# Cache copies moved to a later phase, the last layer norm rewritten, and a projection split between the first attention units

## The chip, the cores and the metric

The kernel runs on one core of a Trainium2 chip. The metric is the device time of one execution in microseconds (us). TensorE (PE) does the matrix products, VectorE (DVE) and ScalarE (ACT) work on rows, GpSimd (POOL) does a little of both and issues DMAs, and SyncE (SP) only issues DMAs. Each engine has its own instruction stream, worked off in order. They meet at semaphores: `wait_ge` holds the stream of its engine until the count is reached.

## The reference

One inference step of a decoder layer, for 1024 prompt rows and 64 sample rows (8 sequences of 8) of width 1024. Cut to what matters here:

```
q, k, v, u, c_b, g_a, g_c = mixer_projections(x, pos, w_in)      # z = x W_in; rotary q, k
A   = dilated_band_attention per group (128,1), (512,4), (2048,16), groups weighted by their denominators
Cv  = c_b * conv3(u)
mix = (sigmoid(g_a) * (A W_pa) + sigmoid(g_c) * (Cv W_pc)) W_out
h   = layer_norm(alpha * x + mix);   y = layer_norm(alpha * h + peer_ffn(h))
new_kv_sample[g] = concat(cache_g, new k/v)[-n_prev:]            # the old rows are moved up by 8
```

The last line matters: of each sample cache (3 groups: 128, 512 and 1024 rows per sequence) all rows but the first 8 are copied unchanged, DRAM to DRAM. That is 52.5 MB.

## The kernel before

The program is a chain of phases, each closed by a barrier over all engines: `load_x`, `prompt_attn`, `sample_attn`, `conv_gates`, `branches`, `mix_ln1`, retrieval, `build_gates`, `experts`, `ln2_out`. Products of the projections are exact to fp32: each factor is split into a high and a low part (ACT writes the high part, DVE the low one), and `split3` (L59 to L61) issues three matmuls for one product.

`prompt_attn` runs over four slices `s` (two heads of each of three groups). In a slice PE first projects: ri = 0, 1, 2 are v, k and q, each for nine row tiles t = 0..8; tile 8 (`PT`) holds the 64 sample rows. A projection is 24 matmuls into one of three PSUM banks, and DVE rotates it (`rotate`: L374, L376, L380) or keeps it; PE turns the prompt tiles (L469). After all 27 projections come 32 units (N: group 0, R: groups 1 and 2). Unit u on PE is `scores` (L483), `turn_probs` (L493), `weigh_values` (L506), issued as scores(u+2), turn_probs(u), weigh_values(u-1). DVE masks the scores (L389) and keeps the outputs (L396), ACT does the exponentials (L308) and copies the turned probabilities (L316). After unit 8 ACT and DVE also split the weights of the next slice (`split_w(s + 1, 0)`: ACT L289 twice, DVE L359 twice); ACT waits there for the load `w_raw`, which SP issues (L223) once the k rows of this slice are stored. So a late `w_raw` holds ACT, and with it the exponentials that PE needs.

The cache copies are DMAs on POOL's queue (L277): two in slice 0, one in slice 1 and one in slice 2, each issued when the slice's last weights are split. Nothing waits for them but the end of the program. The profile calls POOL's DMA queue q0 (software_dynamic) and SP's q1 (hardware_dynamic).

`conv_gates` works through 40 units of weights, five kinds times eight. SP loads `c_raw` (L828, 512 KB for a unit, in pieces of 512 bytes, two buffers); ACT and DVE split it (L854, L884); PE multiplies, 72 matmuls a unit. Unit 0 can't start without the first load, and the next phases can't start before the last unit. POOL stores the finished gates (L840) and gives their buffers free.

`ln2_out` runs over nine row tiles. DVE adds and takes the statistics (L1123, L1127, L1129), ACT the root (L1133), DVE centres and scales (L1139), POOL multiplies by the gain and adds the bias (L1144, L1146) and issues the store (L2108); then POOL itself waits for the store to land before it takes the next tile. Tiles 4 to 8 are first copied to `f_stage` and transposed.

## Time and profile before

| what | value |
|---|---|
| median of 3 runs | 4798.47 us (4792.62 to 4831.89) |
| the profiled execution | 4800.55 us, span 4799.0 us |
| PE busy | 3962.5 us (83%) |
| DVE busy | 3043.2 us (63%) |
| ACT busy | 1179.5 us (25%) |
| POOL busy | 1759.1 us (37%) |
| mean granted TensorE clock | 0.889 of full speed |

The granted clock is 1.00 (2.4 GHz) or 0.50 (1.2 GHz) at any moment; a value between is a mean over a stretch. The busy shares are means over phases with different limits, so the stages that the change touches are read one by one. In the rows below, a timeline row has the start, the length, the engine and line, and in brackets the idle time before it with what ended it; x6 is a count; "PEld" is the loading of weights. A windows row has the stretch and its length, then busy time and count for PE, PEld, DVE, ACT and POOL, then PE's granted clock, the busy share of the 16 DMA engines, and GB/s.

The chain that ended last reaches back only through the last phase, since each phase is closed by a barrier.

### The profile page before, as it was taken

How to read it: one execution, taken by the hardware profiler on the slowest of the kernel's cores; microseconds unless marked ns; L12 is line 12 of the kernel's file. 1: busy time of each engine (PE TensorE's matmuls, PEld its weight loads, DVE VectorE, ACT ScalarE, POOL GpSimd, SP SyncE). 2: the span in 40 equal slices, each digit the busy share in tenths (PEclk: the TensorE clock that was granted, in tenths of full speed). 3: DMA queues.
4: the chain of work that ended last, by engine and by line, in shares of the span. 5: the costliest groups of instructions: out<-in, count | busy, mean ns of one | idle time of the engine just before them, and what ended most of it. 6: DMA issues, size and time to landing. Idle time of an engine off the chain costs nothing. (4 is left out here: it accounts for less than half of the span.)

```text
span 4799.0 us, 64513 instructions
## 1 busy us (share of the span) xinstructions
PE 3962.5 (83%) x24889; PEld 3686.0 (77%) x24889; DVE 3043.2 (63%) x5862; ACT 1179.5 (25%) x2121; POOL 1759.1 (37%) x1228
## 2 busy tenths in 40 slices
PE   7897979798999897798066489888888888888882
PEld 7796969657999896687055488888888888888882
DVE  3332323212222234399888699989998999999984
ACT  1212121311111101143289122222222222222221
POOL 0000000000000002377500566666766666666644
PEclk8787879899999999888589699999999999999996
DMA  5433332252111244110024899999999999999973
GB/s 154 152 99 122 108 113 65 78 218 73 59 60 60 85 130 141 56 31 10 0 124 193 333 359 357 355 350 362 360 355 358 348 359 359 356 356 354 358 271 112
DMA packets 470701, 982.63 MB, mean 205 GB/s; under 512 B 49022, under 2 KB 267518, under 8 KB 467427
## 3 DMA queue, kind: packets, MB, share of 16 engines
q0 software_dynamic: 156704, 619.52, 34.6%
q1 hardware_dynamic: 312578, 355.11, 21.8%
q8 instruction: 166, 2.72, 0.2%
q10 hardware_dynamic: 1152, 4.46, 0.2%
q14 instruction: 101, 0.82, 0.1%
HBM read 901.43 MB, written 131.28 MB: 215 GB/s over the span
## 5 line engine op out<-in xcount | busy, mean ns | idle before, releaser
L1879 POOL DMA_INDIRECT u_row<-in_peer_u_dram,eid x512 | 785.1, 1533 | 703.1 <-DVE dots L1938 417.7
L59 PE MATMUL e_ps<-coef_h,v_h 128*128 128x288 f32 x2048 | 661.3, 323 | 243.6 <-DVE v_l L1907 199.4
L59 PE MATMUL e_ps<-hBh,u_h 128*128 128x288 f32 x2048 | 607.4, 297 | 62.8 <-DVE u_l L1900 62.8
L1954 DVE SCALAR_TENSOR_TENSOR f_row<-v_row,g_coef,f_row 128x1024 f32<-128x1024 f32 x508 | 650.9, 1281 | 6.1 <-DMA v_row<-in_peer_v_dram,eid 5.6
L1885 POOL DMA_INDIRECT v_row<-in_peer_v_dram,eid x512 | 573.1, 1119 | 197.4 <-issue 154.2
L59 PEld LDWEIGHTS e_ps<-coef_h,v_h 128*128 128x128 f32 x2048 | 414.8, 203 | 298.1 <-DVE v_l L1907 244.9
L60 PE MATMUL e_ps<-coef_l,v_h 128*128 128x288 f32 x2048 | 634.4, 310 | 0.0
L61 PE MATMUL e_ps<-coef_h,v_l 128*128 128x288 f32 x2048 | 632.1, 309 | 0.0
L1938 DVE CUSTOM_DVE_ANT_0 u_row<-u_row,h_row 128x1024 f32<-128x1024 f32 x512 | 620.9, 1214 | 10.1 <-DMA u_row<-in_peer_u_dram,eid 10.0
L61 PE MATMUL e_ps<-hBh,u_l 128*128 128x288 f32 x2048 | 607.0, 296 | 0.0
L60 PE MATMUL e_ps<-hBl,u_h 128*128 128x288 f32 x2048 | 606.9, 296 | 0.0
L59 PEld LDWEIGHTS e_ps<-hBh,u_h 128*128 128x128 f32 x2048 | 388.0, 189 | 63.7 <-DVE u_l L1900 63.7
L60 PEld LDWEIGHTS e_ps<-coef_l,v_h 128*128 128x128 f32 x2048 | 415.6, 203 | 0.0
L61 PEld LDWEIGHTS e_ps<-coef_h,v_l 128*128 128x128 f32 x2048 | 414.0, 202 | 0.0
L60 PEld LDWEIGHTS e_ps<-hBl,u_h 128*128 128x128 f32 x2048 | 388.0, 189 | 0.0
L61 PEld LDWEIGHTS e_ps<-hBh,u_l 128*128 128x128 f32 x2048 | 387.8, 189 | 0.0
L59 PE MATMUL c_ps<-xTh,c_wh 128*128 128x384 f32 (+1 forms) x960 | 317.1, 330 | 18.1 <-DVE c_wl L884 18.1
L61 PE MATMUL c_ps<-xTh,c_wl 128*128 128x384 f32 (+1 forms) x960 | 316.3, 329 | 0.0
L60 PE MATMUL c_ps<-xTl,c_wh 128*128 128x384 f32 (+1 forms) x960 | 316.2, 329 | 0.0
L1839 ACT ACTIVATE v_h<-v_raw 128x512 fp32r<-128x512 f32 x256 | 160.3, 626 | 624.1 <-PE e_ps L61 624.1
L281 POOL DMA_DIRECT2D s_att<-attS x4 | 2.3, 571 | 763.3 <-ACT attS L327 763.3
L840 POOL DMA_DIRECT2D s_gate<-gate x16 | 8.5, 531 | 709.6 <-ACT gate L871 709.6
(282 smaller groups left out, 8469.9 us busy)
## 6 DMA issues: line engine op xcount, KB each, us to landing
u_raw<-in_peer_uT_dram SPq DMA_DIRECT2D x128, 512.0 KB, 9.0
v_raw<-in_peer_vQ_dram SPq DMA_DIRECT2D x256, 256.0 KB, 8.5
s_g<-gate_block SPq DMA_DIRECT2D x9, 4096.0 KB, 11.2
x_gate<-s_g SPq DMA_DIRECT2D x64, 576.0 KB
out_o_kv_sample_dram<-in_cache_kv_w_dram POOLq DMA_DIRECT2D x2, 16256.0 KB, 94.6
c_raw<-in_w_in_dram SPq DMA_DIRECT2D x40, 512.0 KB, 3.8
w_raw<-in_w_in_dram SPq DMA_DIRECT2D x96, 192.0 KB, 3.7
cache_v<-in_cache_vS_dram SPq DMA_DIRECT2D x8, 2304.0 KB
```

The source lines that it names most:

```text
L59: pe.matmul(out, lh, rh, start=first, stop=False)
L60: pe.matmul(out, lh, rl, start=False, stop=False)
L61: return pe.matmul(out, ll, rh, start=False, stop=last)
L281: pool.dma_start(io["s_att"][s][:, :SEQ], attS[:]).then_inc(att_out, 16)
L840: pool.dma_start(io["s_gate"][x][j], gate[:, x]).then_inc(gate_out[x], 16)
L1839: act.activation(vh[:, n % 2], vraw[:, n % VR], ACT.Copy).then_inc(v_hi, 1)
L1879: pool.indirect_dma_start(urow[:, r % RING], None, io["peer_u"][0], bass.IndirectOffsetOnAxis(ap=eid[:, r:r + 1], axis=0)).then_inc(urow_i ...
L1885: pool.indirect_dma_start(vrow[:, r % RING], None, io["peer_v"][0], bass.IndirectOffsetOnAxis(ap=eid[:, r:r + 1], axis=0)).then_inc(vrow_i ...
L1938: dve.tensor_tensor_reduce(urow[:, r % RING], urow[:, r % RING], hrow[:, t % 2], 1.0, 0.0, ALU.mult, ALU.add, dots[:, s % 2, x:x + 1]).the ...
L1954: dve.scalar_tensor_tensor(out=f, in0=vrow[:, r % RING], scalar=coef[:, s % 2, x:x + 1], in1=f, op0=ALU.mult, op1=ALU.add).then_inc(weighe ...
```

## The change

Three things.

The cache copies leave `prompt_attn`. All four are issued by POOL, one after the other, as its first act in `conv_gates`. The gate stores there are issued by ACT on its own DMA queue; POOL only waits for them and frees the buffers.

`ln2_out` is written anew. Tiles 4 to 8 come first. All 13 loads are issued ahead, into a buffer for every tile. PE forms alpha * h + f in PSUM, with a scaled identity and the identity (so the transposes of tiles 4 to 8 are part of the sum). DVE takes the statistics from PSUM and does the rest with two `scalar_tensor_tensor` (centre and gain; scale and bias). ACT takes the roots and issues the stores, and waits for them once, at the end. POOL has nothing to do.

In `prompt_attn` the q projection of the sample tile has PSUM bank 7 to itself, and comes in two halves of 12 matmuls: before the turn of q tile 7, and before weigh_values(0). The first scores come between the last prompt projections, and DVE rotates the sample tile after unit 3's step. The outputs of the units have two banks instead of three.

```diff
-    OBANK = (7, 3, 4)
+    OBANK = (3, 4)
+    RING = ZT - 1
...
+        def z_bank(s, ri, t):
+
+            return 7 if (ri, t) == (2, PT) else (s * RING + ri * NT + t) % 3
+
+        def s_bank(s, u):
+            return (s * RING + 2 * NT + PT - SR + u) % SR
...
         def _(pool):
             for s in range(SP):
-                pool.wait_ge(w_lo_done, s * 6 + 6)
-                for g, a, b in ((0, 0, 120), (1, 0, 504)) if s == 0 else ((2, (s - 1) * 508, s * 508),) if s < 3 else ():
-                    pool.dma_start(io[f"o_kv{g}_sample"][0, :, a:b].rearrange("b r w s2 e -> b (r w s2 e)"),
-                                   io[("cache_kv_w128", "cache_kv_w512", "cache_kv_w2048")[g]][0, :, DS + a:DS + b]
-                                   .rearrange("b r w s2 e -> b (r w s2 e)")).then_inc(k["cache_moved"], 16)
                 pool.wait_ge(at_done, 2 * (s + 1))
                 pool.dma_start(io["s_att"][s][:, :SEQ], attS[:]).then_inc(att_out, 16)
...
                     for t in range(PT):
+                        if ri == 2 and t >= PT - 2:
+                            exp(s, t - (PT - 2))
                         copy_turn(s, ri, t)
-                exp(s, 0)
                 for u in range(NU):
-                    if u + 1 < NU:
-                        exp(s, u + 1)
                     copy_probs(s, u)
+                    if u + 2 < NU:
+                        exp(s, u + 2)
...
-                    for t in range(NT):
+                    for t in range(NT if ri == 1 else PT):
                         if t < 2:
                             dve.drain()
+                        if ri == 2 and t == PT - 1:
+                            mask_scores(s, 0)
                         rotate(s, ri, t)
...
-                mask_scores(s, 0)
                 mask_scores(s, 1)
-                for u in range(NU):
+                mask_scores(s, 2)
+                for u in range(1, NU):
                     if u + 2 < NU:
                         mask_scores(s, u + 2)
-                    if u >= 1:
-                        keep_out(s, u - 1)
+                    keep_out(s, u - 1)
+                    if u == 3:
+                        rotate(s, 2, PT)
                     if u == 8 and s + 1 < SP:
                         split_w(s + 1, 0)
...
+            def project(s, ri, t, rows=range(KD)):
                 n, zi = rows_of(t), z_of(s, ri, t)
                 if zi >= 3:
-                    pe.wait_ge(z_free, zi - 2)
+                    pe.wait_ge(z_free, zi - (3 if ri == 0 and t < 3 else 2))
...
+                else:
+                    pe.wait_ge(z_free, z_of(s, 2, PT - SR + u) + 1)
...
-                if u >= 3:
-                    pe.wait_ge(o_kept, s * NU + u - 2)
-                if u == 1:
-                    pe.wait_ge(turn_free, (s + 1) * 2 * PT)
+                if u >= 2:
+                    pe.wait_ge(o_kept, s * NU + u - 1)
+                else:
+                    pe.wait_ge(turn_free, (s + 1) * 2 * PT - 1 + u)
...
+                    for t in range(NT if ri < 2 else PT):
                         project(s, ri, t)
                         if ri == 0 and t == 5 and s >= 1:
                             join(s - 1)
...
                             pe.wait_ge(at_done, 2 * s)
                         if ri >= 1 and t >= 1:
                             turn(s, ri, t - 1)
-                pe.wait_ge(z_free, z_of(s, 2, NT - 1) + 1)
-                scores(s, 0)
-                scores(s, 1)
-                for u in range(NU):
+                        if ri == 2 and t >= PT - 2:
+                            scores(s, t - (PT - 2))
+                project(s, 2, PT, range(KD // 2))
+                turn(s, 2, PT - 1)
+                turn_probs(s, 0)
+                scores(s, 2)
+                project(s, 2, PT, range(KD // 2, KD))
+                weigh_values(s, 0)
+                turn_probs(s, 1)
+                scores(s, 3)
+                for u in range(2, NU):
                     if u + 2 < NU:
                         scores(s, u + 2)
                     if units[u][0] == "R" and units[u - 1][0] == "N":
                         pe.wait_ge(vp_in, 16 * (s + 1))
                     turn_probs(s, u)
-                    if u >= 1:
-                        weigh_values(s, u - 1)
+                    weigh_values(s, u - 1)
                 weigh_values(s, NU - 1)
...
             pool.sem_inc(gate_free, 2)
+            for g, a, b in ((0, 0, 120), (1, 0, 504), (2, 0, 508), (2, 508, 1016)):
+                pool.dma_start(io[f"o_kv{g}_sample"][0, :, a:b].rearrange("b r w s2 e -> b (r w s2 e)"),
+                               io[("cache_kv_w128", "cache_kv_w512", "cache_kv_w2048")[g]][0, :, DS + a:DS + b]
+                               .rearrange("b r w s2 e -> b (r w s2 e)")).then_inc(k["cache_moved"], 16)
             with pool.Fori(0, KD) as j:
-                for x in range(2):
-                    pool.wait_ge(z_act, j * AJ + ((2 + x) * NC + AJ))
-                    pool.dma_start(io["s_gate"][x][j], gate[:, x]).then_inc(gate_out[x], 16)
                 for x in range(2):
                     pool.wait_ge(gate_out[x], (j + 1) * 16)
                     pool.sem_inc(gate_free, 1)
...
+                    if m >= 3:
+                        act.wait_ge(z_act, q * (2 * AJ) + (i // NU * AJ + (m - 1) * NC + AJ))
+                        act.dma_start(io["s_gate"][m - 3][bass.ds(q * 2 + i // NU, 1)].rearrange("o p n -> (o p) n"),
+                                      gate[:, m - 3]).then_inc(gate_out[m - 3], 16)
...
+    ORDER = tuple(range(GTILES, NT)) + tuple(range(GTILES))
+    NY = 4
...
+            for i, t in enumerate(ORDER):
+                n = rows_of(t)
+                sp.dma_start(H[:n, t], io["s_h"][t * P:t * P + n]).then_inc(h_in[t], 16)
                 if t < GTILES:
+                    sp.dma_start(F[:, t], io["s_f"][t * P:(t + 1) * P]).then_inc(h_in[t], 16)
...
+        @block.tensor
+        def _(pe):
+            pe.wait_ge(alpha_ready, 1)
+            for i, t in enumerate(ORDER):
+                n = rows_of(t)
+                if i >= NY:
+                    pe.wait_ge(centred, i - NY + 1)
+                pe.wait_ge(h_in[t], 32 if t < GTILES else 16)
+                for a in range(2):
+                    cols = slice(a * 512, (a + 1) * 512)
+                    pe.matmul(ps[:n, i % NY, cols], scaled_id[:n, :n], H[:n, t, cols], start=True, stop=False)
+                    if t < GTILES:
+                        m = pe.matmul(ps[:n, i % NY, cols], k["ident"][:], F[:, t, cols], start=False, stop=True)
+                    else:
+                        for j in range(4 * a, 4 * a + 4):
+                            m = pe.matmul(ps[:n, i % NY, j * P:(j + 1) * P], k["acc"][:, j, t * P - TA:t * P - TA + n],
+                                          k["ident"][:], start=False, stop=(j % 4 == 3))
+                m.then_inc(y_ready, 1)
...
+            def stats(i):
+                n, x = rows_of(ORDER[i]), i % 2
+                dve.wait_ge(y_ready, i + 1)
+                for a in range(2):
+                    dve.bn_stats(st[:n, x, 6 * a:6 * a + 6], ps[:n, i % NY, 512 * a:512 * (a + 1)])
+                dve.drain()
+                dve.bn_aggr(mv[:n, x], st[:n, x]).then_inc(var_ready, 1)
+
+            def finish(i):
+                t, x = ORDER[i], i % 2
+                n = rows_of(t)
+                dve.wait_ge(std_ready, i + 1)
+                dve.reciprocal(rstd[:n, x:x + 1], std[:n, x:x + 1])
+                dve.scalar_tensor_tensor(out=H[:n, t], in0=ps[:n, i % NY], scalar=mv[:n, x, 0:1], in1=gain[:n],
+                                         op0=ALU.subtract, op1=ALU.mult).then_inc(centred, 1)
+                dve.drain()
+                dve.scalar_tensor_tensor(out=H[:n, t], in0=H[:n, t], scalar=rstd[:n, x:x + 1], in1=bias[:n],
+                                         op0=ALU.mult, op1=ALU.add).then_inc(done, 1)
+
+            stats(0)
+            dve.wait_ge(consts, 32)
+            for i in range(NT):
+                if i + 1 < NT:
+                    stats(i + 1)
+                finish(i)
...
+            def root(i):
+                n, x = rows_of(ORDER[i]), i % 2
+                act.wait_ge(var_ready, i + 1)
+                act.activation(std[:n, x:x + 1], mv[:n, x, 1:2], ACT.Sqrt, bias=eps[:n]).then_inc(std_ready, 1)
+
+            def store(i):
+                t = ORDER[i]
+                dst = io["o_y_prompt"][0, t * P:(t + 1) * P] if t < PT else io["o_y_sample"].rearrange("b s d -> (b s) d")
+                act.wait_ge(done, i + 1)
+                act.dma_start(dst, H[:rows_of(t), t]).then_inc(y_out, 16)
+
+            root(0)
+            for i in range(NT):
+                if i + 1 < NT:
+                    root(i + 1)
+                store(i)
+            act.wait_ge(y_out, 16 * NT)
```

The body of `ln2_out` before (the class `Norm`, the staging and POOL's part) goes; it stands with the kernel above.

Where instructions move on POOL, from the start of `prompt_attn` to the head of the loop in `conv_gates`. Before (8x32x16256 is 256 pieces of 65,024 bytes; QB is in `sample_attn`):

```order
L277 DMA out_o_kv_sample_dram<-in_cache_kv_w_dram 8x8x15360
L277 DMA out_o_kv_sample_dram<-in_cache_kv_w_dram 8x32x16128
L281 DMA s_att<-attS 128x1024
L277 DMA out_o_kv_sample_dram<-in_cache_kv_w_dram 8x32x16256
L281 DMA s_att<-attS 128x1024
L277 DMA out_o_kv_sample_dram<-in_cache_kv_w_dram 8x32x16256
L281 DMA s_att<-attS 128x1024 x2
```

The same stretch of POOL after the change:

```order
L284 DMA s_att<-attS 128x1024 x4
L157 UNCONDITIONAL_BRANCH
L639 UNCONDITIONAL_BRANCH
L641 MEMSET QB 128x960
L577 UNCONDITIONAL_BRANCH
L850 UNCONDITIONAL_BRANCH
L854 DMA out_o_kv_sample_dram<-in_cache_kv_w_dram 8x8x15360
L854 DMA out_o_kv_sample_dram<-in_cache_kv_w_dram 8x32x16128
L854 DMA out_o_kv_sample_dram<-in_cache_kv_w_dram 8x32x16256 x2
L857 UNCONDITIONAL_BRANCH
```

The four copies have moved past `sample_attn` and stand together ahead of the loop.

PE in slice 0, from the last matmuls of the sample tile (64x384) to the first units, before (L469 turns q tile 7, L483 scores, L493 turns probabilities, L506 weighs values):

```order
L59 MATMUL a_ps<-w_parts,xTh 64x384
L60 MATMUL a_ps<-w_parts,xTh 64x384
L61 MATMUL a_ps<-w_parts,xTl 64x384
L469 MATMUL a_ps<-ident,qR 128x128 x3
L483 MATMUL a_ps<-kT,qT 128x128 x2
L483 MATMUL a_ps<-kT,qT 128x256
L493 MATMUL a_ps<-ident,S 128x128
L483 MATMUL a_ps<-kT,qT 128x256
L493 MATMUL a_ps<-ident,S 128x128
L506 MATMUL a_ps<-vR,PTs 128x64
```

PE at the same place after the change; the left-out rows are more of the two halves:

```order
L61 MATMUL a_ps<-w_parts,xTl 64x384
L477 MATMUL a_ps<-ident,qR 128x128 x3
L503 MATMUL a_ps<-ident,S 128x128
L493 MATMUL a_ps<-kT,qT 128x256
L59 MATMUL a_ps<-w_parts,xTh 64x384
...
L61 MATMUL a_ps<-w_parts,xTl 64x384
L516 MATMUL a_ps<-vR,PTs 128x64
L503 MATMUL a_ps<-ident,S 128x128
L493 MATMUL a_ps<-kT,qT 128x256 x2
```

The first two scores have gone ahead, and twelve matmuls of the sample tile lie on either side of the first turned probabilities.

ACT around unit 8 of slice 0 before (L308 exponential, L316 copy, L289 split of the next slice's weights):

```order
L316 ACTIVATE PTs<-a_ps 128x256
L308 ACTIVATE S,stat<-S,stat 128x256
L316 ACTIVATE PTs<-a_ps 128x256
L289 ACTIVATE w_parts<-w_raw 128x1536 x2
L308 ACTIVATE S,stat<-S,stat 128x256
L316 ACTIVATE PTs<-a_ps 128x256
```

And after:

```order
L311 ACTIVATE S,stat<-S,stat 128x256
L319 ACTIVATE PTs<-a_ps 128x256
L311 ACTIVATE S,stat<-S,stat 128x256
L292 ACTIVATE w_parts<-w_raw 128x1536 x2
L319 ACTIVATE PTs<-a_ps 128x256
L311 ACTIVATE S,stat<-S,stat 128x256
```

The split has one exponential more ahead of it, and is still two activations in one piece.

## Rows read from the trace of the kernel before

**Rows 1.** Waits, 0 to 1000 us: waiter, releaser, total us, times, longest.

```profile
PE a_ps L493 <- ACT S L308: 66.6, 7, 27.9
```

**Rows 2.** Timeline of PE, slice 0: start, us, work [idle before, releaser].

```profile
165.77 0.92 PE L483 MATMUL a_ps<-kT,qT 64*128 64x128 f32 x6 [0.84 <-DVE qR L376]
...
167.17 0.33 PE L493 MATMUL a_ps<-ident,S 128*128 128x128 f32 x1 [0.48 <-ACT S L308]
...
202.22 0.69 PE L493 MATMUL a_ps<-ident,S 128*128 128x128 f32 x2 [12.54 <-ACT S L308]
```

**Rows 3.** Windows: length, busy us (x count) by engine, PE clock, DMA share, GB/s.

```profile
168.00:271.70 103.70, 91.16 (x323) 71.43 (x323) 24.79 (x91) 32.47 (x93) 0.00 (x0) 0.50 0.21 72
395.50:409.80 14.30, 13.78 (x76) 9.29 (x76) 6.61 (x31) 8.06 (x29) 0.00 (x0) 1.00 0.52 202
437.70:507.20 69.50, 69.48 (x255) 56.80 (x256) 17.30 (x66) 22.32 (x65) 0.00 (x0) 0.50 0.04 5
863.00:915.10 52.10, 51.55 (x330) 40.61 (x330) 23.01 (x97) 31.19 (x96) 0.00 (x0) 1.00 0.06 8
877.30:915.10 37.80, 37.73 (x254) 31.24 (x254) 15.75 (x63) 21.77 (x62) 0.00 (x0) 1.00 0.04 2
```

**Rows 4.** Timeline of DVE and ACT, slice 1, around unit 8.

```profile
407.09 0.42 DVE L389 CUSTOM_DVE_ANT_0 S<-a_ps,mask 128x256 f32<-128x256 f32 x1 [0.40 <-PE a_ps L483]
...
433.41 1.48 ACT L289 ACTIVATE w_parts<-w_raw 128x1536 fp32r<-128x1536 f32 x1 [25.57 <-DMA w_raw<-in_w_in_dram]
...
434.93 1.76 DVE L359 TENSOR_TENSOR w_parts<-w_raw,w_parts 128x1536 fp32r<-128x1536 f32 x1 [26.85 <-ACT w_parts L289]
```

**Rows 5.** Page, part 5: POOL's gate stores: busy us, mean ns | idle before.

```profile
L840 POOL DMA_DIRECT2D s_gate<-gate x16 | 8.5, 531 | 709.6 <-ACT gate L871 709.6
```

**Rows 6.** DMA issues: transfer, queue, count, KB each, median us to landing.

```profile
out_o_kv_sample_dram<-in_cache_kv_w_dram POOLq DMA_DIRECT2D x2, 16256.0 KB, 94.6
...
c_raw<-in_w_in_dram SPq DMA_DIRECT2D x40, 512.0 KB, 3.8
...
out_o_kv_sample_dram<-in_cache_kv_w_dram POOLq DMA_DIRECT2D x1, 16128.0 KB, 90.3
...
out_o_kv_sample_dram<-in_cache_kv_w_dram POOLq DMA_DIRECT2D x1, 3840.0 KB, 28.7
```

**Rows 7.** Timeline of POOL's and SP's queues, slice 2.

```profile
567.78 0.68 POOL L277 DMA_DIRECT2D out_o_kv_sample_dram<-in_cache_kv_w_dram  x1 [29.40 <-DVE w_parts L359]
...
594.82 69.05 SPq L223 DMA_DIRECT2D w_raw<-in_w_in_dram  x8
```

**Rows 8.** DMA queues, 372 to 420 us: packets, MB, share of 16 engines.

```profile
q0 software_dynamic: 138, 8.97, 50.0%
q1 hardware_dynamic: 139, 0.06, 0.5%
```

**Rows 9.** Windows: both copies of slice 0 under way.

```profile
104.00:128.00 24.00, 24.00 (x144) 22.92 (x143) 8.20 (x20) 2.76 (x10) 0.03 (x1) 1.00 1.04 310
```

**Rows 10.** Line L828, SP: duration ns min/median/max, first and last start us.

```profile
L828 SPq DMA_DIRECT2D c_raw<-in_w_in_dram x40: 372/373/429, 1146.6 to 1606.0; - x40
```

**Rows 11.** Timeline of PE: the first matmul of conv_gates.

```profile
1154.27 0.68 PE L59 MATMUL c_ps<-xTh,c_wh 128*128 128x384 f32 x1 [5.44 <-DVE c_wl L884]
```

**Rows 12.** Chain of waits, last phase: start us, us, what.

```profile
4704.77 0.05 issue
...
4751.62 2.96 DMA out_o_y_prompt_dram<-n_y
...
4759.82 2.95 DMA out_o_y_prompt_dram<-n_y
...
4794.58 0.59 POOL out_o_y_sample_dram L2108
```

**Rows 13.** Groups of instructions, 4704 to 4800 us: busy us, mean ns.

```profile
L1127 DVE BATCH_NORM_STATS2 n_st<-n_y 128x6 f32<-128x512 f32 x16 | 10.3, 685 | 0.7
...
L2120 PE MATMUL f_ps<-ident,f_stage 128*128 128x128 f32 x32 | 7.9, 428 | 57.4 <-ACT f_stage L2081 57.4
...
L1123 DVE SCALAR_TENSOR_TENSOR n_y<-n_res,f_ps 128x1024 f32<-128x1024 f32 x4 | 4.9, 1221 | 11.1 <-POOLq L2110 11.1
...
L1129 DVE BATCH_NORM_AGGREGATE n_mv<-n_st 128x2 f32<-128x12 f32 x8 | 1.7, 209 | 0.6
```

98 lines of the change are left out of this document (29 added, 69 removed).

## The prediction

> **What bounds the kernel now.** The waits come first. In the attention over the prompt PE waits 66.6 us for ACT's exponentials, in seven waits, the longest 27.9 us [rows 1]. Four of them are the 0.48 us ahead of each slice's first turned probabilities, as in slice 0 [rows 2]; the other three, 66.6 - 4 x 0.48 = 64.7 us, follow unit 8 in slices 0, 1 and 2 (12.54 us in slice 0 [rows 2]). The timeline names what is behind them: ACT stands at the split of the next weights, 25.57 us for `w_raw` in slice 1 [rows 4]. The queues tell why that is late. In slice 2 the copy is issued at 567.78 and takes 94.6 us [rows 6, 7], so it lands at 662.4; SP's eight `w_raw` DMAs are issued at 594.82 and their issue ends 69.05 us later, at 663.9 [rows 7]. The loads move when the copy is over.
>
> The windows add the clock. Slice 3 has no copy ahead of it and no split in it: its units take 52.1 us, all at a granted clock of 1.00 (2.4 GHz). In slice 1 the units run at 1.00 until the stall, and afterwards 69.5 us at 0.50 (1.2 GHz), for work that takes 37.8 us in slice 3; slice 0 is at 0.50 from 168 us to the end of its units [rows 3]. At 0.50 these units never brought the clock back.
>
> The last phase is bound by one chain: POOL's two passes, and the landing of each store, for which POOL waits, 8.20 us a tile (4751.62 to 4759.82) [rows 12]. From 4704.77 to the span's end it takes 94.2 us. `conv_gates` is bound by PE: 40 loads are issued between 1146.6 and 1606.0, one in 11.8 us [rows 10], and a load lands in 3.8 us [rows 6], so no load is late there today.
>
> **The change, part by part.** *Copies out of the attention.* The three stalls of 64.7 us go. A smaller one takes their place, since the split itself stays in the streams. ACT then needs 2 x 1.48 us, DVE 2 x 1.76 us behind it, the first at most 1.5 us after ACT begins [rows 4], about 1.5 + 1.5 + 1.76 = 4.8 us from ACT's start to DVE's end. Laid over the 1.39 us rhythm of units at full clock (14.3 us for the ten steps up to the stall [rows 3], the first ones shorter), PE waits about 1.5 us for the copy of unit 9's probabilities and about 1.9 us for unit 11's mask and exponential: 3.4 us a slice. So 64.7 - 3 x 3.4 = 54.5 us are saved. Slice 0 gains more: it reached its stall at 202.22 - 12.54 = 189.7, 23.9 us after its first scores at 165.77 [rows 2], where slice 1 needed 14.3 us [rows 3]; with a full clock at the start that is another 9.6 us. A unit more is done at full clock before the second pause, 69.5 - 37.8 = 31.7 us over 22 units or 1.4 us each, and two of them: about 1 us a slice, 3 us. Sum: **-67 us**.
>
> Whether the clock outlives the pause decides much more. In slice 0 it fell at 168 us, right after waits of 0.84 and 0.48 us [rows 2]; slices 1 and 3 began with the same two waits and stayed at 1.00 [rows 3]. The new pause is 3.4 us in about 4.5 us. That is nearer to the case in which it fell, so I take it as falling, in each of slices 0 to 2, and the rest of their units at 0.50 as before. The other end: it stays, and the rest takes 37.8 us instead of 69.5, less the 1 us already counted, about 30 us a slice, 92 us in all.
>
> *The sample tile's projection in two halves.* The 24 matmuls are the same and at the same clock; they now cover the 0.84 + 0.48 = 1.32 us that PE waits in each slice [rows 2]: 4 x 1.32 = **-5 us**. The rotation of that tile now lies behind unit 3 on DVE, some 1.8 us; DVE is idle 0.40 us ahead of each mask alone [rows 4] and works under half of the time in slice 3 (23.01 of 52.1 us [rows 3]), so at most a few tenths show. The third output bank was slack: with two, weigh_values(u) waits for keep_out(u-2), which DVE does a unit earlier. Taken at nothing.
>
> *The gate stores on ACT.* POOL spends 8.5 us on the sixteen issues today [rows 5]; ACT works 1179.5 us in the whole span, and in `conv_gates` PE is the bound. If that cover were gone, it would be these 8.5 us. Taken at nothing.
>
> *The copies in `conv_gates`.* This is the big term. All four are issued as the phase begins, beside the first `c_raw` load, and nothing is computed before that load. What a copy does to such a load: from 372 to 420 us, with one copy under way, 138 pieces passed on POOL's queue (8.97 MB, 65 KB each) and 139 on SP's (0.06 MB, up to 512 bytes each), and the copy filled 50.0% of the 16 engines [rows 8]. That is one small piece for one large piece, on half of the engines. With both copies of slice 0 under way the share was 1.04 at 310 GB/s [rows 9]: the second copy had the other half. So four copies fill both halves: 28.7 + 94.6 = 123.3 us on one, 90.3 + 94.6 = 184.9 us on the other [rows 6], 32 + 32 = 64 large pieces per engine of the latter. A `c_raw` load is 1024 pieces of 512 bytes, by 16 engines 64 each. One for one, 64 small pieces pass just with the last of the 64 large ones. So the first load lands at about 1146 + 184.9 = 1331 instead of 1146.6 + 3.8 = 1150.4, **+180 us**; PE's first matmul, at 1154.27 today [rows 11], comes at about 1334. The second load lands right behind, and from there on the phase runs as it did. What bounds it: nothing, if the loads pass freely; 308.2 us (the sum of the four landings) less one unit, 11.8, less the 3.8 us, some 292 us, if all four copies share one half.
>
> Here the Trainium skill says something else than the rows (DMA: Bandwidth & Descriptors, "Queues, rings and completion order"): an engine goes round its queues packet by packet, and a packet is typically 9 to 17 descriptors. Were only the small pieces gathered so, 64 would need 4 to 8 turns, and by this estimate the load would take some 20 us. The trace has 139 beside 138, so the sum goes by one for one.
>
> *The last phase.* POOL's passes, and the waits for the stores, go. DVE then has two statistics of 0.685, an aggregate of 0.209, a reciprocal no longer than that, and two full passes of 1.221 us [rows 13]: 1.37 + 0.21 + 0.2 + 2.44 = 4.2 us, with the small gaps 4.5 us a tile. PE has, at the clock of today, eight products of 128 columns (7.9 us for 32, or 2.0 us) and two of 512, of four times the columns, 2.0 us: 4.0 us, below DVE; at 5.5 us it would cost 9 us more. All loads are ahead. Start: about 1 us to issue, a 512 KB load of 3.8 us [rows 6] and the first sum of 4.0 us make 9 us; nine tiles 40.5 us; the last store, from 4794.58 to 4799.0 today [rows 12], 4.4 us; 1 us for the rest. 94.2 - 55 = **-39 us**, with -30 and -44 as ends.
>
> **Sum.** 4800.5 - 67 - 5 + 180 - 39 = 4869.5 us against the profiled execution. That lies 2.1 us above the median of the runs (4798.47), so **4867 us**.
>
> **The rivals.**
> 1. *The clock survives the pause* in the units. For it: slices 1 and 3 passed 1.32 us of waiting. Against it: slice 0 fell at that. 4867 - 92 = 4775 us for all three slices, 4806 for two, 4836 for one. Chance 0.15.
> 2. *The loads are not held up in `conv_gates`*, the other side: the first `c_raw` pieces get through, and the later ones too. For it: before a queue fills up, the half of the engines without a copy passes small pieces freely. Against it: four copies leave no half free for 123 us, and 138 to 139 is plain. 4867 - 180 = 4687 us. It decides from the point at which the first load lands less than about 60 us late: below that the kernel is faster by over 1%. Chance 0.08. A milder form: eight small pieces pass for each large one. A large one takes 48 us x 8 engines / 138 = 2.8 us [rows 8], eight turns 22 us, and the sum would be 4687 + 22 = 4709 us. Chance 0.04. That is the packet rule of the Trainium skill's page above.
> 3. *All copies on one half*: 4867 + (292 - 180) = 4979 us. For it: the rows don't say which half the third copy takes. Against it: the 1.04 of the first two. Chance 0.05.
> 4. *The copies hold up less than thought at the start*: the first load gets in ahead of them, and the second is the one that waits. PE does unit 0 meanwhile: 11.8 us less, 4855. This lies in the forecast.
>
> **How the numbers follow.** My forecast, with rival 4, has 0.66; its own range is 4840 to 4895 (the last phase -30 to -44, the copies up to 11 us longer where both halves are busy, rival 4). Rival 1 adds the part down to 4775. From 4770 to 4900 this makes 0.81. Outside stay rivals 2 and 3 and 0.02 for the rest. A difference of 1% is about what a measurement can tell from none: 48 us. Slower by over 1% (above 4846): forecast 0.64 and rival 3, 0.05, some 0.70. Within 1%: rival 1 and the low edge of the forecast, 0.18. Faster: rival 2, 0.12.
>
> **What would show it.** In the profile after: no wait for `w_raw` in the attention, and waits of PE for ACT of 1.5 to 2 us after unit 8, with the clock at 0.50 behind them; units of some 86 us in slices 0 to 2 instead of 105 to 112. The first matmul of `conv_gates` some 180 us after the phase's first load, not 8; the four copies landing within 190 us; and after that 11.8 us a unit. A last phase of some 55 us with DVE busy nearly throughout. The prediction is wrong above all if that first matmul comes early, or if the units of slices 0 to 2 show 1.00 throughout.

## The result, and the profile after

The changed kernel takes 4894.1 us (median, 4883.4 to 4899.4) beside 4814.9 for the kernel before: a ratio of 1.018 [1.013, 1.023]. It is slower, as forecast, and by more than the likeliest value (4867). In the profiled executions the difference is larger, 4896.4 against 4799.0 us of span, +97.4, where the prediction's terms made +69. The terms below are read between profiled executions; one phase with the same work differs between two executions by some 10 us (an example is in (1) below), so no term is known better than that.

Cut at SyncE's first DMA of a phase, the two traces give:

| from, to | before | after | difference | predicted |
|---|---|---|---|---|
| start to the gate projection (`conv_gates`) | 1145.5 | 1072.5 | -73.0 | -72 |
| `conv_gates`, to its state store | 507.1 | 724.8 | +217.8 | +180 |
| from there to the last norm | 3052.2 | 3045.8 | -6.4 | 0 |
| last norm | 94.2 | 53.3 | -40.9 | -39 |

Three sums are as forecast; that of `conv_gates` is 38 us larger. The first of the three agrees by two errors of opposite sign, as the experiments show.

**Attention.** Windows of the kernel after: the units of slice 0 up to the split of the next weights and behind it, then behind the splits of slices 1 and 2, and slice 3, which has no split (columns as in [rows 3]).

```profile
159.00:172.00 13.00, 13.00 (x75) 9.12 (x73) 6.57 (x27) 6.21 (x23) 0.00 (x0) 1.00 0.00 1
172.00:250.00 78.00, 75.29 (x291) 61.08 (x291) 21.55 (x77) 27.99 (x78) 0.00 (x0) 0.55 0.06 9
380.00:460.00 80.00, 77.69 (x297) 62.80 (x297) 21.81 (x80) 28.65 (x81) 0.00 (x0) 0.55 0.08 15
590.00:668.00 78.00, 75.83 (x287) 61.36 (x288) 21.10 (x75) 27.29 (x75) 0.00 (x0) 0.54 0.07 13
780.00:850.00 70.00, 62.12 (x391) 50.02 (x391) 30.59 (x117) 33.05 (x103) 0.00 (x0) 0.95 0.05 6
```

Its waits of PE from 0 to 1000 us, the two of the units (columns as in [rows 1]):

```profile
PE a_ps L516 <- ACT PTs L319: 3.6, 3, 1.2
PE a_ps L503 <- ACT S L311: 3.6, 3, 1.5
```

The 66.6 us of [rows 1] are gone. What is left of them is a pause of about 2.4 us in each of three slices, and each time the clock falls from 1.00 to 0.5 behind it. The prediction said this, with a pause of 3.4 us.

**`conv_gates`.** PE's matmuls that a late weight load held up:

```profile
1204.18 0.68 PE L59 MATMUL c_ps<-xTh,c_wh 128*128 128x384 f32 x1 [128.47 <-DVE c_wl L905]
1247.49 0.68 PE L59 MATMUL c_ps<-xTh,c_wh 128*128 128x384 f32 x1 [29.56 <-DVE c_wl L905]
1318.76 0.68 PE L59 MATMUL c_ps<-xTh,c_wh 128*128 128x384 f32 x1 [57.03 <-DVE c_wl L905]
```

Against one wait of 5.44 us [rows 11] there are three while the copies run, 215.1 us. The DMA queues from 1110 to 1160 us (packets, MB, share of the 16 engines):

```profile
q0 software_dynamic: 189, 12.24, 98.7%
q1 hardware_dynamic: 188, 0.10, 0.7%
```

and from 1200 to 1210 us:

```profile
q0 software_dynamic: 304, 2.08, 86.9%
q1 hardware_dynamic: 297, 0.15, 8.1%
```

The first pair is [rows 8] once more, on all 16 engines: one load piece of 512 bytes for one copy piece of 65 KB. A large piece now holds its engine for 50 us x 16 / 189 = 4.2 us; with one copy under way it was 2.8 us (48 us x 8 engines / 138, from [rows 8]). The second pair is a stretch in which a copy ends. The 2.08 MB are 32 large pieces, and some 270 more packets of q0 carry next to nothing. The load's pieces go one for one with those too, so in this kernel the stretch in which a copy ends lets a burst of load pieces through. But these packets are not the end of the copy. Where nothing is ahead of it, they come right behind a copy's issue: in the kernel before, q0 has no packet from 565 to 568 us, the copy is issued at 567.78 [rows 7], and the next two microseconds are the first row here. The last copy of the kernel after lands without them (1312 to 1316 us, second row):

```profile
q0 software_dynamic: 271, 0.46, 85.1%
...
q0 software_dynamic: 11, 0.20, 11.4%
```

So each copy brings its own, and in the kernel after they seem to wait for the copy ahead; the profile does not say to which copy a packet belongs. The copies' own rows (KB each, median us to landing):

```profile
out_o_kv_sample_dram<-in_cache_kv_w_dram POOLq DMA_DIRECT2D x2, 16256.0 KB, 203.7
...
out_o_kv_sample_dram<-in_cache_kv_w_dram POOLq DMA_DIRECT2D x1, 16128.0 KB, 133.4
...
out_o_kv_sample_dram<-in_cache_kv_w_dram POOLq DMA_DIRECT2D x1, 3840.0 KB, 28.9
```

**Last norm.** Groups of instructions of the last 53 us: DVE starts a tile every 4.07 us for most of the phase (its L2136 at 4863.15 and 4867.23, for one), with next to no gaps; the forecast was 4.5.

```profile
L2127 DVE BATCH_NORM_STATS2 n_st<-f_ps 128x6 f32<-128x512 f32 (+1 forms) x18 | 11.6, 685 | 12.5 <-PE f_ps L2114 12.5
L2139 DVE SCALAR_TENSOR_TENSOR f_h<-f_h,n_rstd,n_bias 128x1024 f32<-128x1024 f32 (+1 forms) x9 | 11.6, 1283 | 0.8
...
L2136 DVE SCALAR_TENSOR_TENSOR f_h<-f_ps,n_mv,n_gain 128x1024 f32<-128x1024 f32 (+1 forms) x9 | 11.4, 1264 | 0.0
...
L2129 DVE BATCH_NORM_AGGREGATE n_mv<-n_st 128x2 f32<-128x12 f32 (+1 forms) x9 | 1.9, 208 | 0.7
```

### The profile page after: what moved, and what is told of

It is laid out like the page before. It is cut to its first block and busy times, and to the rows that moved or that the text cites. A ratio compares the mean times of both kernels' runs of the same rounds, so it can differ in the third digit from the quotient of the medians.

```text
span 4896.4 us, 64660 instructions
## 1 busy us (share of the span) xinstructions
PE 3977.6 (81%) x24981; PEld 3692.1 (75%) x24981; DVE 3029.9 (62%) x5863; ACT 1174.8 (24%) x2116; POOL 1700.4 (35%) x1185
## 5 line engine op out<-in xcount | busy, mean ns | idle before, releaser
L59 PEld LDWEIGHTS c_ps<-xTh,c_wh 128*128 128x128 f32 x960 | 184.5, 192 | 232.2 <-issue 202.4
L905 DVE TENSOR_TENSOR c_wl<-c_raw,c_wh 128x1024 fp32r<-128x1024 f32 x40 | 48.7, 1224 | 480.3 <-ACT c_wh L871 477.8
## 6 DMA issues: line engine op xcount, KB each, us to landing
out_o_kv_sample_dram<-in_cache_kv_w_dram POOLq DMA_DIRECT2D x2, 16256.0 KB, 203.7
```

Of the source, the lines that this page charges most:

```text
L59: pe.matmul(out, lh, rh, start=first, stop=False)
L905: dve.tensor_tensor(wl[:, i % 2], raw[:, i % 2], wh[:, i % 2].bitcast(F32), ALU.subtract).then_inc(w_lo, 1)
```

## The experiments: the change in parts

**Copies and gate stores alone.** The kernel before, with the GpSimd copies taken out of the attention and `conv_gates` as changed.

```
 # prompt attention, GpSimd: the wait and the copies are taken out
-                pool.wait_ge(w_lo_done, s * 6 + 6)
-                for g, a, b in ((0, 0, 120), (1, 0, 504)) if s == 0 else ((2, (s - 1) * 508, s * 508),) if s < 3 else ():
-                    pool.dma_start(...).then_inc(k["cache_moved"], 16)
 # conv_gates as in the changed kernel
+            for g, a, b in ((0, 0, 120), (1, 0, 504), (2, 0, 508), (2, 508, 1016)):
+                pool.dma_start(...).then_inc(k["cache_moved"], 16)
```

> The kernel before with one part of the change: the cache copies and the gate stores moved (prompt attention and last norm as before). Theory on record, with the size that the changed kernel showed: the three stalls of the attention go and three short pauses come (-54 to -65), the copies beside the gate projection's loads cost about 207, so 140 to 155 above before, near 4955. Rival, that the copies cost less beside the old attention because the phase meets them in another state: 100 to 130 above. If the change's loss came from another part, this kernel is within 50 of before.

Measured: 4985.1 (4943.9 to 4991.5), 1.034 [1.027, 1.042] of before, so +166, above the 140 to 155 expected. The copies cost 207.5 us here, as expected; what they give back in the attention is less (table below).

**The last norm alone** (`ln2_out` of the changed kernel, all else before's).

> The kernel before with the new last norm alone. Theory: the last phase goes from 94.2 to about 53 us, so 41 below before, about 4774. Rival: the short last phase is only short because the experts before it end otherwise in the changed kernel; then less than 25 below.

Measured: 4776.4, ratio 0.992 [0.988, 0.995], -42 against a median of 4818.9 (now of 19 runs): as forecast.

**The projection alone** (the changed prompt attention, with before's copies in it).

```
 # GpSimd, in the changed attention: before's copies are back
             for s in range(SP):
+                pool.wait_ge(w_lo_done, s * 6 + 6)
+                for g, a, b in ((0, 0, 120), (1, 0, 504)) if s == 0 else ((2, (s - 1) * 508, s * 508),) if s < 3 else ():
+                    pool.dma_start(...).then_inc(k["cache_moved"], 16)
```

> The kernel before with the reordered sample projection alone; the copies stay where they were. Theory: 5 to 15 below before, and the clock after the stall is low as before. Rival: the clock is kept in some slices in which it fell before; then 30 or more below.

Measured: 4781.3 (4768.3 to 4792.0), ratio 0.994 [0.991, 0.997], -38. The 5 to 15 expected were too few, and the rival's number came.

**The changed kernel without the copies.**

```
-            for g, a, b in ((0, 0, 120), (1, 0, 504), (2, 0, 508), (2, 508, 1016)):
-                pool.dma_start(...).then_inc(k["cache_moved"], 16)
 # at the program's end
-                act.wait_ge(k["cache_moved"], 16 * (NG + 1))
```

> The changed kernel without the four cache copies (that part of the outputs is left out). Theory: the gate projection then takes 475 us or less in place of 678, the whole 200 to 210 below the changed kernel, about 4690. Rival, that the gate stores on ScalarE's queue or the new placement carry part of the loss: the phase stays 20 or more above before's 459.

Measured: 4683.2, ratio 0.974 [0.969, 0.979], as expected. The four traces against before and after, in us, from GpSimd's four stores of a finished slice and SyncE's first DMAs:

| kernel | slices 0 to 2 end | slice 3 takes | `conv_gates` starts | `conv_gates` takes |
|---|---|---|---|---|
| before | 769.8 | 159.4 | 1145.5 | 507.1 |
| last norm alone (attention as before) | 760.6 | 197.3 | 1168.5 | 507.9 |
| copies alone | 716.2 | 199.0 | 1126.5 | 714.6 |
| projection alone | 750.8 | 158.9 | 1123.6 | 506.8 |
| after | 696.7 | 158.7 | 1072.5 | 724.8 |
| after, no copies | 697.2 | 158.5 | 1070.8 | 511.8 |

What follows.

(1) *The copies' term* is 724.8 - 511.8 = 213 us in the changed kernel, 714.6 - 507.1 = 207.5 alone; the gate stores and all else add 4.8. With the same copies the kernel of "The split in eight pieces" below has 714.9 in this phase, which makes 203.

(2) *Slices 0 to 2.* The copies' leaving is worth 44 to 54 us, the projection 10 to 20, both together 64 to 73. The forecast had this sum right and gave the projection too little. The trace of the copies alone shows why. The old order has the waits of 0.84 and 0.48 us ahead of each slice's first units [rows 2], and in this trace the clock falls right there in all four slices, where before's own trace kept it in slices 1 and 3. In slice 1:

```profile
380.00:385.00 5.00, 4.51 (x14) 2.55 (x13) 1.87 (x11) 2.62 (x11) 0.00 (x0) 0.61 0.23 59
385.00:390.00 5.00, 5.00 (x17) 3.49 (x16) 1.32 (x6) 2.14 (x8) 0.00 (x0) 0.50 0.00 0
```

The kernel after has no such wait, and the first units run at 1.00 until the pause behind unit 8 (159 to 172 us above). So the full clock at a slice's start, for which the prediction gave slice 0 9.6 us as a part of the copies' leaving, is kept by the new order.

(3) *Slice 3* takes either 159 us or 197 to 199, for the same work. Four traces have the old order of the projection: before has the short slice, the last norm alone, the copies alone and "Small pieces where the copies were" below (197.5) have the long one. The same 1.33 us of waiting stand ahead of its first units in all four; the clock outlives them in before (first row) and not in the others (the second and third row are those of the small pieces):

```profile
860.00:866.00 6.00, 4.67 (x27) 3.09 (x26) 3.03 (x13) 2.54 (x11) 0.00 (x0) 1.00 0.12 31
...
800.00:820.00 20.00, 18.67 (x112) 16.55 (x111) 7.61 (x23) 3.67 (x14) 0.00 (x0) 1.00 0.02 5
820.00:840.00 20.00, 20.00 (x66) 13.87 (x65) 5.70 (x26) 7.33 (x28) 0.00 (x0) 0.50 0.04 11
```

With the new order slice 3 takes 158 to 159 us in every trace. So part of what the projection is worth, up to 38 us, lies there, and the prediction did not have it: it compared with one profiled execution that happened to have the short slice. The spread of the runs fits this (4778 to 4831 over 19 runs of before, 4768 to 4792 over 10 of the projection alone), but how often an unprofiled run has the long slice is not known.

## The experiments: what a copy does to a load

**Pieces of 4 KB.** The same bytes at the same place; every second row, so that rows don't join into large pieces.

```
-            for g, a, b in ((0, 0, 120), (1, 0, 504), (2, 0, 508), (2, 508, 1016)):
-                pool.dma_start(io[f"o_kv{g}_sample"][0, :, a:b].rearrange("b r w s2 e -> b (r w s2 e)"),
+            for g, rows in ((0, 120), (1, 504), (2, 1016)):
+                for a in range(0, rows, 256):
+                    b = min(a + 256, rows)
+                    for r in range(2):
+                        pool.dma_start(io[f"o_kv{g}_sample"][0, :, a + r:b:2].rearrange("b r w s2 e -> b r (w s2 e)"),
```

> The changed kernel with the same copies in pieces of 4 KB in place of 64 KB (every second row of a cache, so that pieces don't join), in 14 transfers. Theory one for one: a load's piece waits for one copy piece, now 16 times shorter (4.2 us becomes about 0.26), a load of 64 pieces an engine takes 17 to 20 us; against 11.8 us of work a unit that loses some 60 to 90 in 220 us of copies, so 4750 to 4785 in place of 4894. Rival, bytes: the copies take the engines' time in proportion to what they have to move, whatever the size of a piece; then the loss stays near 207 and the time near 4890.

Measured: 4706.0 (4698.6 to 4710.8), ratio 0.979 [0.973, 0.985]. The term fell from 213 us to 533.8 - 511.8 = 22. The queues of this kernel from 1110 to 1160 us:

```profile
q0 software_dynamic: 6687, 13.54, 82.3%
q1 hardware_dynamic: 4161, 2.10, 15.7%
```

The copies move 10% more than before in these 50 us (13.54 against 12.24 MB), and the loads 21 times as much. 2.10 MB are four loads of 512 KB, one in 12.5 us, where a unit of work needs 11.8 [rows 10]. So it was hardly the bytes that were in each other's way; it was the turns. The forecast, 4750 to 4785, had scaled 4.2 us down to 0.26 and a load to 17 us or more, and was too high.

**Pieces of 16 KB**, four rows each, otherwise like that.

```
+                        pool.dma_start(io[f"o_kv{g}_sample"][0, :, a:b].rearrange("b (r y x) w s2 e -> y b r (x w s2 e)", y=2, x=4)[r],
```

> The changed kernel with the same copies in pieces of 16 KB, in 14 transfers. Theory one for one: a piece pair takes 1.05 us, a load of 64 pieces an engine 67 us; in the 215 us that the copies take some 4 units run in place of 18, so a loss of 140 to 175 against the kernel without copies (4683): 4825 to 4860. Rival: what costs is only pieces of 64 KB, and at 16 KB the loads are as hidden as at 4 KB: 4705 to 4730.

Measured: 4855.5, ratio 1.009 [1.006, 1.012]: within the forecast, a loss of 172 against the kernel without copies. Its queues from 1150 to 1170 us:

```profile
q0 software_dynamic: 244, 4.00, 95.6%
q1 hardware_dynamic: 244, 0.12, 2.2%
```

and PE's waits for late weights in `conv_gates`:

```profile
PE c_ps L59 <- DVE c_wl L908: 186.9, 9, 47.0
```

244 for 244, and a pair in 20 us x 16 / 244 = 1.31 us (I had 1.05). By the length of the phase (687.3 us here) three sizes now stand: 64 KB 213, 16 KB 176, 4 KB 22 us. The loss does not grow with the size in proportion. With copies of some 240 us it reads as their duration less the units that get through meanwhile, so it is near the whole duration for any piece that makes a load much longer than a unit, and almost nothing once a load takes about as long as one.

**One copy after the other.**

```
+            for i, (g, a, b) in enumerate(((0, 0, 120), (1, 0, 504), (2, 0, 508), (2, 508, 1016))):
+                if i:
+                    pool.wait_ge(k["cache_moved"], 16 * i)
```

> The changed kernel with each copy issued only when the one before it has landed. Theory: one copy holds one half of the engines at 2.8 us a large piece, its pieces still go one for one with the loads', which need every engine; the copies take 28.7 + 90.3 + 94.6 + 94.6 = 308 or a little more, in which two or three units run; the loss is about 270 to 290, so near 4965. Rival: with half of the engines free and shorter pieces the loads go through quicker (64 pieces at 2.8 in place of 4.2 us); then the loss is 207 or less, 4890 or under.

Measured: 4897.6 (4892.2 to 4902.2), the same as after (4894.1): far from the theory (4965), and 8 us above the rival's 4890 or under. Its queues from 1110 to 1160 us:

```profile
q0 software_dynamic: 168, 10.84, 50.0%
q1 hardware_dynamic: 168, 0.09, 0.6%
```

and its two largest copies, in the DMA issues:

```profile
out_o_kv_sample_dram<-in_cache_kv_w_dram POOLq DMA_DIRECT2D x2, 16256.0 KB, 90.6
```

Again one for one, now 50 us x 8 / 168 = 2.4 us a piece, and a copy lands in 90.6 us, not 203.7. So two copies side by side slow each other: together they moved 12.24 MB in 50 us, 245 GB/s, this one alone 10.84 MB, 217 GB/s. The four landings sum to 283 us; what this loses against side by side (240 us, from 1073 to about 1314) seems to come back where one copy ends and the next begins: there the load that stood behind it is set free. PE works for 18.2 of the 22 us from 1173, where the second copy lands and the third is issued, and for 7.7 of the 68 us behind them; no run tests this separately.

**The copies after the first two loads.**

```
+            for x in range(2):
+                pool.wait_ge(raw_in[x], 16)
```

> The changed kernel with the copies issued once the gate projection's first two loads have landed. Theory: the first wait of 128 falls away, two units (24 us) run under the copies, and the later waits stay; 20 to 30 less, near 4870. Rival: the later loads wait for the same copies, the end is set by when the copies end, and the gain is under 10.

Measured: 4879.6, 15 less than after, between the two forecasts (20 to 30 less, under 10 less).

## The experiments: the clock, and other places for the copies

**The split in eight pieces.** In the changed kernel, ScalarE and VectorE split the next slice's weights in 128x384 pieces, one a unit, in place of two halves after unit 8.

```
 # ScalarE
-                    if u == 8 and s + 1 < SP:
-                        split_w(s + 1, 0)
+                    if 8 <= u < 16 and s + 1 < SP:
+                        split_piece(s + 1, u - 8)
 # VectorE
+                    if 13 <= u < 21 and s + 1 < SP:
+                        split_piece(s + 1, u - 13)
```

> The changed kernel with the next slice's weight split cut into eight pieces, one per unit (ScalarE after units 8 to 15, VectorE after 13 to 20), in place of two long instructions in a row after unit 8. Theory: it is this pause that drops TensorE's clock from 1.00 to about 0.55 over the units that follow in slices 0 to 2; without it the clock stays up as in slice 3 (0.95), each of the three slices takes some 45 us less (208.4 against 158.7), so 100 to 140 less, 4755 to 4795. Rival: the units' own thin work drops the clock and only slice 3 escapes; then under 15 less.

Measured: 4785.3 (4777.8 to 4791.3), ratio 0.994 [0.992, 0.997], and 109 less than after. Its windows over the same stretches as those of after:

```profile
172.00:250.00 78.00, 78.00 (x497) 69.72 (x498) 29.60 (x101) 32.29 (x91) 0.72 (x1) 1.00 0.13 33
380.00:460.00 80.00, 80.00 (x495) 77.98 (x495) 28.08 (x58) 15.14 (x28) 0.56 (x1) 1.00 0.29 85
590.00:668.00 78.00, 78.00 (x467) 75.74 (x467) 30.89 (x63) 13.63 (x30) 0.53 (x1) 1.00 0.25 79
```

and one piece between an output's copy and a mask, on DVE:

```profile
183.04 0.22 DVE L414 COPY O_kept<-a_ps 128x64 f32<-128x64 f32 x1 [0.33 <-PE a_ps L530]
183.18 0.55 DVE L375 TENSOR_TENSOR w_parts<-w_raw,w_parts 128x384 fp32r<-128x384 f32 x1
183.68 0.42 DVE L407 CUSTOM_DVE_ANT_0 S<-a_ps,mask 128x256 f32<-128x256 f32 x1
```

The clock stays at 1.00, and a slice takes 173.6 us in place of 208.4. So it was a pause of 2.4 us that made the clock fall, and the clock that made the units slow. This is the size that rival 1 had put at 92 us; it is shown by taking the pause away, and has the three pauses themselves in it, some 7 us.

**The copies in the retrieval**, where the page of the kernel after shows 9 and 1 GB/s in two slices of 122 us; behind the last weight load, 64 KB pieces, five transfers.

```
 # retrieve, GpSimd, ahead of queries(HEADS - 2)
+                    for x in range(2):
+                        pool.wait_ge(raw_in[x], HEADS * 16)
+                    for g, a, b in ((0, 0, 120), (1, 0, 504), (2, 0, 350), (2, 350, 666), (2, 666, 1016)):
+                        pool.dma_start(...).then_inc(k["cache_moved"], 16)
```

> The changed kernel with the copies (64 KB pieces, in five transfers that share the two halves equally) issued in the retrieval, behind its last weight load, where the trace shows 200 us with next to nothing on the DMA engines. Theory: nothing is queued behind them there, so the time is that of the changed kernel without copies, 4683, plus up to 10: about 4690. Rival: they reach into the expert loads that follow, or the retrieval's small transfers wait; 4720 or more.

> As c1_copies_in_retrieve, and the weight split in eight pieces as in b4_split_in_pieces. The two gains lie in different phases and add: 4690 less 109 is about 4580. Rival: the gain in the attention is given back by a clock that falls later; 4620 or more.

Measured: 4853.5 and, with the split in pieces, 4753.2 (0.989 [0.983, 0.995]). Both theories, 4690 and 4580, failed. The two changes add (100 of 109 us), but the copies cost 170 us, at a place where no load waits for them. GpSimd's timeline:

```profile
2155.62 3.40 POOL L1458 DMA_DIRECT2D out_o_kv_sample_dram<-in_cache_kv_w_dram  x5
...
2376.97 2.58 POOL L1482 TENSOR_TENSOR q_hot<-q_hot 128x1152 f32<-128x1152 f32 x1 [187.93 <-issue]
```

The copies are issued at 2155.6, 221 us later they are over, and in between GpSimd stands for 187.9 us at L1482, ahead of which the program has `pool.drain()`.

**No drain.** The same kernel, with a semaphore in its place.

```
-                                       ALU.mult)
-                    pool.drain()
+                                       ALU.mult).then_inc(multed, 1)
+                    pool.wait_ge(multed, h * 2 + (x + 1))
```

> As c1_copies_in_retrieve, but GpSimd's drain between the multiplication and the sum is replaced by a semaphore that it raises and waits for itself. Theory: the drain waits for GpSimd's own transfers; without it 4685 to 4700. Rival: GpSimd stands still for another reason, and the time stays near 4853.

Measured: 4722.7 (4717.8 to 4727.3), ratio 0.983 [0.978, 0.988]: 131 of the 170 us are back, and it is 23 us above what was expected. GpSimd's drain waits for the transfers that GpSimd has issued. The remaining 39 stand here, at VectorE's first instruction of the next phase:

```profile
2376.74 0.69 DVE L1675 SCALAR_TENSOR_TENSOR eid_f<-sel 128x512 f32<-128x512 f32 x1 [33.98 <-PEq L1324]
```

All engines wait for TensorE's sequencer, and it arrives as the copies end. In the kernel without copies the same wait is 0.41 us. That its instructions came late behind the copies is likely, and is not shown.

**The copies from SyncE**, behind its last weight load of the retrieval, and the split in pieces.

```
                     sp.dma_start(raw[:, x], w_view[x, h]).then_inc(raw_in[x], 16)
+            for g, a, b in ((0, 0, 120), (1, 0, 504), (2, 0, 350), (2, 350, 666), (2, 666, 1016)):
+                sp.dma_start(...).then_inc(k["cache_moved"], 16)
```

> As c2_pieces_and_retrieve (64 KB pieces, in the retrieval), but issued by SyncE behind its last weight load. Theory: it is GpSimd that stood still for 187 us since it had issued the copies itself; from SyncE they cost nothing, 4683 less 98 to 109, so 4575 to 4590. Rival: the copies cost the retrieval the same from any queue: near 4750.

Measured: 4623.0 (0.961 [0.957, 0.967]), between the forecast (4575 to 4590) and the rival. GpSimd goes on, TensorE's sequencer is in time, but SyncE's next small load is behind the copies on its own queue:

```profile
2282.16 2.36 DVE L1703 TENSOR_TENSOR hot<-count,selT 128x1024 f32<-128x1024 f32 x2 [34.54 <-DMA count<-in_c_count_dram]
```

These 34.5 us are most of the 33 to 48 by which it misses its forecast.

**Small pieces where the copies were.** The kernel before, its copies cut into 4 KB pieces and nothing else:

```
+                    for a in range(a0, b0, 256):
+                        b = min(a + 256, b0)
+                        for r in range(2):
+                            pool.dma_start(io[f"o_kv{g}_sample"][0, :, a + r:b:2].rearrange("b r w s2 e -> b r (w s2 e)"),
```

> The kernel before, copies where they were in the attention, only cut into pieces of 4 KB. Theory: the weight loads behind them no longer wait for a large piece each, so the three stalls (12 to 28 us) go without a move, and with them what a1_copies_in_conv gained in the attention (about 43): 4775, and with the copies' cost elsewhere nothing. Rival, that the loads wait for the copies' bytes: the stalls stay and the time is within 10 of before.

Measured: 4776.0, ratio 0.990 [0.986, 0.993], -43: as forecast. Waits of PE, 0 to 1000 us:

```profile
PE a_ps L496 <- ACT S L311: 11.4, 6, 9.2
```

Of the 66.6 us [rows 1], 11.4 are left: to take away the stalls of the attention, the copies did not have to be moved. The changed kernel with these copies in the attention and the split in pieces:

> The changed kernel with the copies back at their old place in the attention, in pieces of 4 KB, and the weight split in eight pieces. Theory: no stall there and the clock stays up, the gate projection has no copies beside it: 4575 to 4600. Rival: the copies slow the slices' loads enough for the clock to fall in one of them: 4620 or more.

Measured: 4675.2 (4645.4 to 4686.6), ratio 0.972 [0.965, 0.978]: above the 4575 to 4600 expected, as the rival had it. ScalarE waits a little for the weights in slice 0, and the clock falls behind that (its windows):

```profile
160.00:180.00 20.00, 20.00 (x117) 14.52 (x116) 9.61 (x41) 10.88 (x39) 0.00 (x0) 1.00 1.02 293
180.00:200.00 20.00, 18.89 (x88) 15.45 (x87) 8.70 (x35) 10.92 (x36) 0.00 (x0) 0.67 0.21 48
```

PE was idle for 1.1 us of those 20. In slices 1 and 2 it was 5.7 and 3.0 (380 to 400 and 580 to 600 us), and the 20 us behind them are at 0.50.

**The best version** keeps the copies beside `conv_gates`, in 4 KB pieces, and splits the weights in eight.

> The changed kernel with copies in 4 KB pieces beside the gate projection and the weight split in eight pieces: 4706 less 109, about 4597, if the two add.

Measured: 4605.4 (4599.6 to 4610.8; 4597 expected), ratio 0.958 [0.953, 0.964]: 214 us, 4.2%, below before, and 289 below the changed kernel. PE is busy for 591.6 of the 600 us from 150 to 750:

```profile
150.00:750.00 600.00, 591.62 (x3619) 535.81 (x3617) 242.96 (x715) 186.66 (x536) 1.81 (x3) 0.99 0.17 47
```

## Why the prediction was right in sign and short in size

- **Copies out of the attention, -67, and the projection, -5.** The sum, -72, measured -73.0, in part by luck. What held: no stall, a pause of 2.4 us (3.4 forecast), the clock at 0.5 behind it. What did not: the split between the two, 44 to 54 and 10 to 20 us over slices 0 to 2. The prediction credited the full clock at slice 0's start to the copies and took the reordered projection only for the 1.32 us of waiting that it covers. With the copies alone moved, the clock fell behind those 1.32 us in every slice; with the new order they are gone, and it stayed.
- **Gate stores, 0.** All that is not the copies adds 4.8 us to the phase.
- **Copies in `conv_gates`, +180: the step that failed.** It measured +213 (203 to 213 over the traces). One for one was right, to the packet (189 to 188). Wrong was what followed from it, that the first load waits 180 us and nothing waits after it. The first wait of PE was 128.5 us, 123 more than before, so 57 less than forecast; two more waits followed, 29.6 and 57.0 us, which the forecast had at nothing. Three readings led there. First, the copies' duration was taken as the 184.9 us that a half needs while the other is mostly quiet. With both under way a large piece takes 4.2 us, not 2.8, and the copies last 240 us. The 1.04 at 310 GB/s of [rows 9] already stood below twice the 187 GB/s that one copy makes (8.97 MB in 48 us [rows 8]), and I read of it only that the second half was in use. Second, "64 small pieces pass just with the last of the 64 large" was wrong: some 540 packets of SyncE's queue passed in the first 4 us (1073 to 1077) beside 83 of the copies', and each end of a copy let a burst through. Third, "from there on the phase runs as it did" was wrong: loads stood behind large pieces to the end of the last copy. Of the 240 us, some two units' work was saved.
- **The range.** The terms that the prediction names for its own range, added to 4867, reach from about 4850 to 4887; the edges of 4840 and 4895 have no term behind them. A longer duration of the copies stood in it with 11 us, and measured 55.
- **Last norm, -39.** -40.9 in the trace, -42 alone.
- **Rival 2 and the packet rule.** The Trainium skill (DMA: Bandwidth & Descriptors, "Queues, rings and completion order") has an engine take a packet of typically 9 to 17 descriptors in a turn. The queues of after, of the serial copies and of the 16 KB pieces show one for one (188, 168 and 244), so the trace does not agree for these transfers, and rival 2 fell.
- **Rival 1.** The clock did not survive the pause. What it would be worth, 92 us by the forecast, is 109 by the run that takes the pause away, some 7 of them the pauses themselves.
- **The base.** 4798.5 was the median of three runs; more of them have 4815 to 4820. That fits slice 3, which comes in two lengths, 38 us apart: the profiled execution of before has the short one, which also fits a difference of +97 between the traces and +79 between the medians.

## What to carry to other kernels

Two transfers that share a DMA engine take turns by piece, so look at the size of a bulk copy's pieces before moving the copy: 4 KB in place of 64 KB took its price from 213 to 22 us. A bulk transfer finds its price in what is queued behind it anywhere: in small loads on the same engines, in a drain of the engine that issued it, in the next load on its own queue. Where TensorE's work is thin, cut long side work on the other engines into pieces that fit between two of its instructions; a pause of 2.4 us cost 35 us a slice, by the clock that fell behind it. And profile more than one execution of the kernel before: a phase that comes in two lengths makes one trace a poor base.

## What the runs showed of the hardware

- A copy's pieces and a load's pieces on the same engines took turns one for one, at 64 KB (189 to 188, and 168 to 168 with one copy) and at 16 KB (244 to 244) against pieces of 512 bytes.
- A GpSimd drain waits for the transfers that GpSimd itself issued: 187.9 us, gone with a semaphore in its place.
- In 64 KB pieces a copy between two places in DRAM moved 187 GB/s (kernel before) and 217 GB/s (copies one after the other) on half of the engines, and two moved 245 on all 16; in 4 KB pieces it was 13.54 MB in 50 us, 271 GB/s, with 42 GB/s of loads beside it. The large pieces brought nothing.
- A large copy comes with some 270 packets that carry next to nothing. They ran within 2 us of the issue where nothing was ahead, and they take turns like any other.
- The granted clock fell to 0.5 within a slice behind pauses of 1.1 to 2.4 us in the units, and stayed at 1.00 through three slices without them. The same 1.33 us ahead of slice 3's first units left it at 1.00 in one trace and not in three.
- Under 221 us of large copies, TensorE's sequencer came 34 us late into the next phase.
